# Expert-choice layers: the last expert's round written out, its rows added on chip, the layer norm of all tiles inside it

## What is computed

```python
mix = windowed_gqa_sink(x, ...)            # layer 0
mix = bidir_rglru_block(x, ...)            # layer 1
x = layer_norm(ALPHA * x + mix, ln_mix_g[layer], ln_mix_b[layer])
ffn = expert_choice_moe(x, w_router, w_gate_up, w_down)
x = layer_norm(ALPHA * x + ffn, ln_ffn_g[layer], ln_ffn_b[layer])
```

```python
def expert_choice_moe(x, w_router, w_gate_up, w_down):
    aff = jax.nn.softmax((x @ w_router).astype(jnp.float32), axis=-1)
    gates, idx = lax.top_k(jnp.swapaxes(aff, 1, 2), cap)      # cap = 128 rows for each of 16 experts
    xs = x[bi, idx]
    g, u = jnp.split(jnp.einsum('becd,edf->becf', xs, w_gate_up), 2, axis=-1)
    out = jnp.einsum('becf,efd->becd', jax.nn.silu(g) * u, w_down) * gates[..., None]
    return jnp.zeros_like(x).at[bi, idx].add(out)
```

## Time and profile before

| | |
|---|---|
| median of 3 runs | 4730.37 us (4727.5 to 4732.37) |
| the profiled execution | 4735.36 us, its span 4733.2 us |
| mean granted TensorE clock | 0.949 |
| TensorE busy | 4216.9 us (89%), 23090 records |
| VectorE, ScalarE, GpSimd busy | 1578.3 us (33%), 1068.2 us (23%), 267.2 us (6%) |
| products of layer 0's experts, L2867 and L2893 | 444.5 and 223.4 us |
| products of layer 1's experts, L2867 and L2893 | 444.0 and 223.4 us |

### The profile page before, as it was taken

The page is one execution under the profiler, slowest core; times in us unless marked ns, Lnnn a source line. Parts: engine busy times, 40 slices in busy tenths (PEclk is TensorE's granted clock), DMA queues, the critical chain, the costliest instruction groups (busy, mean ns, idle before and its releaser), DMA issues. The chain is left out here.

```text
span 4733.2 us, 61819 instructions
## 1 busy us (share of the span) xinstructions
PE 4216.9 (89%) x23090; PEld 2186.2 (46%) x23091; DVE 1578.3 (33%) x2933; ACT 1068.2 (23%) x1827; POOL 267.2 (6%) x304
## 2 busy tenths in 40 slices
PE   7899996888999979979899599999699995999995
PEld 4555444776444544434455244444344452444442
DVE  3355354443401232223574410110256444011102
ACT  1155222443200001111363100000246331000002
POOL 0000001221000010010000000000000000000000
PEclk8899998999999989989999799999799997999998
DMA  2040244333212289961104488888511144888884
GB/s 94 22 182 10 62 173 120 82 81 97 86 36 72 85 320 358 358 241 63 46 4 167 159 312 308 311 313 312 167 48 37 54 169 162 309 309 313 312 307 163
DMA packets 416663, 807.16 MB, mean 171 GB/s; under 512 B 140624, under 2 KB 280784, under 8 KB 383568
## 3 DMA queue, kind: packets, MB, share of 16 engines
q1 hardware_dynamic: 387392, 702.80, 42.4%
q0 software_dynamic: 16704, 60.82, 4.7%
q10 hardware_dynamic: 12368, 40.70, 2.2%
HBM read 682.60 MB, written 121.63 MB: 170 GB/s over the span
## 5 line engine op out<-in xcount | busy, mean ns | idle before, releaser
L2867 PE MATMUL ec0e_pg<-ec_wg,ec0e_xT 128*128 128x512 f32 x1024 | 444.5, 595 | 2.1 <-DVE ec0e_xT L2920 2.1
L2867 PE MATMUL ec1e_pg<-ec_wg,ec1e_xT 128*128 128x512 f32 x1024 | 444.0, 594 | 2.1 <-DVE ec1e_xT L2920 2.1
L2867 PEld LDWEIGHTS ec0e_pg<-ec_wg,ec0e_xT 128*128 128x128 f32 x1024 | 195.4, 191 | 248.3 <-issue 248.3
L2867 PEld LDWEIGHTS ec1e_pg<-ec_wg,ec1e_xT 128*128 128x128 f32 x1024 | 195.2, 191 | 248.1 <-issue 248.1
L1385 PE MATMUL mix_pb<-h_h_all,mix_wg 128*128 128x512 f32 x512 | 224.6, 598 | 8.8 <-DMA mix_wg<-in_w_in_dram 8.8
L3151 PE MATMUL lrui_pA<-lrui_xT,lrui_w 128*128 128x512 f32 x512 | 223.7, 597 | 2.6 <-ACT lrui_xT L3225 2.6
L2893 PE MATMUL ec1e_py<-lru_wd,ec1e_hidT 128*128 128x512 f32 x512 | 223.4, 594 | 0.0
L2893 PE MATMUL ec0e_py<-gqa_wd,ec0e_hidT 128*128 128x512 f32 x512 | 223.4, 594 | 0.0
L679 PE MATMUL front_pz<-h_h_all,front_w 128*128 128x512 f32 x480 | 211.6, 599 | 8.8 <-DMA front_ones<-in_head_ones_dram 8.8
L2908 ACT ACTIVATE ec1e_sg<-ec1e_pg 128x512 f32<-128x512 f32 x32 | 19.1, 598 | 649.7 <-PE ec1e_pg L2867 649.7
L2908 ACT ACTIVATE ec0e_sg<-ec0e_pg 128x512 f32<-128x512 f32 x32 | 19.1, 598 | 648.3 <-PE ec0e_pg L2867 648.3
(11 more groups left out here) (550 smaller groups left out, 6251.9 us busy)
## 6 DMA issues: line engine op xcount, KB each, us to landing
ec_wg<-in_moe_w_gate_up_dram SPq DMA_DIRECT2D x256, 1024.0 KB, 6.3
gqa_wd<-in_moe_w_down_dram SPq DMA_DIRECT2D x128, 512.0 KB, 4.4
lru_wd<-in_moe_w_down_dram SPq DMA_DIRECT2D x128, 512.0 KB, 4.4
moe_wb<-in_w_dram SPq DMA_DIRECT2D x32, 1024.0 KB, 14.1
h_h_all<-in_w_dram SPq DMA_DIRECT2D x32, 1024.0 KB, 13.9
wkv_inp<-arrays SPq DMA_DIRECT2D x160, 128.0 KB, 2.8
arrays<-front_out SPq DMA_DIRECT2D x36, 512.0 KB, 5.7
yb<-mlaa_zero SPq DMA_DIRECT2D x1, 16384.0 KB
```

The costliest lines, as they stand in the source:

```text
L2867: return nc.tensor.matmul(pg[:, b, :], xT[:, k, :], wg[:, k, b * HALF:(b + 1) * HALF], start=k == 0, stop=k == KD - 1)
```

## The change

What it does, part by part:
- A new class `Layers` holds what both layers and both of their ends use: the identity, one buffer of eight tiles (`aT`, the former `oT` and `ggT`), the weights `wd`, the norm's vectors `gb`, and the small tiles `rows`, `old`, `place`, `small`, `at`.
- The loop of `choice_phase` runs over 15 experts, and the round of expert 15 (LAST) is written out behind it on every engine. In all rounds TensorE's `turn_hid(1)` now stands in front of k = 2 of the down product. The last round has no `turn_x`, and there is no 17th gather.
- When the scatter of expert 14 has landed, SP loads the eight tiles of `acc_dram`, and GpSimd gathers expert 15's 128 rows of `acc_dram` into `rows` (in layer 0 also into `old`). ScalarE and VectorE norm the eight tiles in place (layer 0: `old` as a ninth) around the steps of the last round; SP stores them. Expert 15's contribution isn't in these tiles.
- VectorE then adds py * gate to `rows` (L3091). In layer 1 these rows are normed into `fixed`, and GpSimd stores them over the output's rows when the tiles' stores have landed. In layer 0 that is done in `lru_mix`: `fixed_rows` norms them, `change` = `fixed` − normed `old`, and TensorE adds the change to `xT` by 16 matmuls with `place`, a matrix of 0 and 1 (a row of it has its 1 at the token of that row). It is made from the new input `steps`. TensorE turns the eight tiles straight from SBUF.
- `norm_phase` is gone, and with it the norm, the reload and the stores in `lru_mix`.

```diff
 choice_phase
+    LAST, R, FIRST, MIDDLE = E2 - 1, NT + 1, 3, 4
+    ALL = NT if end else NT + 1
...
             sync
+                sp.wait_ge(sent, E2)
+                for t in range(NT):
+                    sp.dma_start(tile(t), acc_dram[t * P:(t + 1) * P, :]).then_inc(tile_in[t], 16)
+                for t in range(NT):
+                    sp.wait_ge(o_ready, t + 1)
+                    sp.dma_start(out_dram[t * P:(t + 1) * P, :], tile(t)).then_inc(tile_out, 16)
             gpsimd
-                with pool.Fori(0, E2 // 2) as i:
+                with pool.Fori(0, E2 // 2 - 1) as i:
...
+                gather(1)
+                pool.wait_ge(y_ready, E2)
+                pool.indirect_dma_start(acc_dram, bass.IndirectOffsetOnAxis(ap=ic[0][:, :], axis=0), y[:, :], None, compute_op=ALU.add).then_inc(added, 16)
+                pool.wait_ge(added, 16 * LAST)
+                pool.sem_inc(sent, 1)
+                pool.indirect_dma_start(rows[:, :], None, acc_dram, bass.IndirectOffsetOnAxis(ap=at_last[:, :], axis=0)).then_inc(rows_in, 16)
+                if not end:
+                    pool.indirect_dma_start(old[:, :], None, acc_dram, bass.IndirectOffsetOnAxis(ap=at_last[:, :], axis=0)).then_inc(old_in, 16)
+                pool.wait_ge(x_in, 16 * E2)
+                if end:
+                    pool.wait_ge(fix_ready, 1)
+                    pool.wait_ge(tile_out, NO)
+                    pool.indirect_dma_start(out_dram, bass.IndirectOffsetOnAxis(ap=at_last[:, :], axis=0), fixed[:, :], None).then_inc(fix_out, 16)
+                    pool.wait_ge(fix_out, 16)
             tensor
-                    E.hold(x_in, e * 16 + 32)
-                    turn_x()
-                    turn_hid(1)
+                    if more:
+                        E.hold(x_in, e * 16 + 32)
+                        turn_x()
                     E.hold(y_ready, last(e))
                     for k in range(KD):
+                        if k == 2:
+                            turn_hid(1)
                         E.hold(wd_in[k], now(e, 16))
...
+                with pe.Fori(0, LAST) as e:
+                    one_expert(e, True)
+                one_expert(LAST, False)
             scalar
+                top(LAST)
+                for t in range(FIRST):
+                    stats(t)
+                silu_half(LAST, 0)
+                for t in range(FIRST, MIDDLE):
+                    stats(t)
+                silu_half(LAST, 1)
+                keep_hid(LAST)
+                for t in range(MIDDLE):
+                    roots(t)
+                for t in range(MIDDLE, ALL):
+                    stats(t)
+                    roots(t)
             vector
+                def norm(t, other=None):
+                    dve.wait_ge(sum_done, t + 1)
+                    mean(t, t)
+                    if other is not None:
+                        scaled(other)
+                    mean_squares(t, t)
+                    centred(tile(t), tile(t), t)
...
+                for t in range(FIRST):
+                    norm(t)
+                gated(LAST, 0)
+                for t in range(FIRST, MIDDLE):
+                    norm(t)
+                gated(LAST, 1)
+                keep_hid(LAST)
+                for t in range(MIDDLE, ALL):
+                    norm(t, t - MIDDLE)
+                dve.wait_ge(rows_in, 16)
+                dve.wait_ge(d_used, now(LAST, KD, KD))
+                nc.vector.scalar_tensor_tensor(rows[:, :], py[:, :], gate[:, LAST:LAST + 1], rows[:, :], ALU.mult, ALU.add,
+                                               accum_out=small[:, R, 0:1]).then_inc(rows_ready, 1)
+                rest = range(ALL - MIDDLE, ALL)
+                if end:
...
+                    centred(fixed[:, :], rows[:, :], R)
+                    mean_squares(ALL, R)
+                    scaled(rest[0])
...
+                    nc.vector.scalar_tensor_tensor(fixed[:, :], fixed[:, :], small[:, R, 5:6], gb[:, 1, :], ALU.mult, ALU.add).then_inc(fix_ready, 1)
+                    rest = rest[1:]
+                for t in rest:
+                    scaled(t)
 lru_mix
             tensor
+            def changed(k):
+                if k >= 2:
+                    pe.wait_ge(xT_ready, k - 1)
+                for h in range(2):
+                    m = nc.tensor.matmul(pA[:, 2 * (k % 2) + h, :], change[:, k * P:(k + 1) * P], place[:, halves[h]], start=True, stop=True)
+                m.then_inc(c_psum, 1)
...
-                pe.wait_ge(xT_ready, 4 * h + 4)
+                pe.wait_ge(xT_ready, KD)
...
-            for t in range(4):
+            for t in range(NT):
                 turn(t)
-            branch(0, 0)
...
+            pe.wait_ge(change_ready, 1)
+            for k in range(KD):
+                changed(k)
+            for i in range(2):
+                branch(i, 0)
+                branch(i, 1)
             vector
+            fixed_rows()
+            for k in range(KD):
+                keep_change(k)
```

More of the change, by code:

```diff
@@ L2773, in _, with choice_phase, tile @@
             nc.vector.tensor_copy(gate[:, :], pl[:, E2:2 * E2])
-def choice_phase(nc, name, ident, x_dram, acc_dram, gate, idx, weights, ln_ffn=None, gb=None, gb_in=None):
+def choice_phase(nc, name, layers, x_dram, acc_dram, gate, idx, weights, ln_ffn, out_dram, steps, end):
+    LAST, R, FIRST, MIDDLE = E2 - 1, NT + 1, 3, 4
+    ident, tiles, gb, rows, old, place, small, at_last = (layers.ident, layers.aT, layers.gb, layers.rows, layers.old, layers.place, layers.small,
+                                                          layers.at)
+    gb_in, tile_out = layers.gb_in, layers.tile_out
+    NG = 32 * (2 if end else 1)
+    NO = 16 * NT * (2 if end else 1)
+    ALL = NT if end else NT + 1
+    def tile(t):
+        return tiles[:, t, :] if t < NT else old[:, :]
     with Phase(nc, name) as ph:
@@ L2788, in choice_phase @@
         warm = ph.sb("warm", [P, 1])
+        junk = ph.sb("junk", [P, D])
+        fixed = ph.sb("fixed", [P, D]) if end else None
         pg = ph.ps("pg", [P, 4, HALF])
@@ L2932, in _ @@
                     keep_x()
[L2933 to L2935 removed]
+                    keep_hid(e)
                     V.hold(d_used, now(e, KD))
```

365 lines of the change are left out of this document (167 added, 198 removed).

## The result

The changed kernel takes **4672.19 us** (median of 4 runs, 4668.46 to 4675.37), beside 4731.37 us of the kernel before (4 runs, 4727.5 to 4736.96). The ratio is 0.9874, with a 95% interval of 0.9857 to 0.9891: 59 us faster, between 52 and 68. The forecast was 4685 us, a gain of 45 us. The sign was right; the size was 14 us short. The time lies 0.2 us above the low end of the range, 4672. The kernel before, executed beside it, was itself 1 us longer than the 4730.37 that the forecast started from. By the gain, 59.2 us against the 58.4 of the low end, the result lies 0.8 us outside.

A forecast was written before the change was run, and what follows sets the result against it. TensorE time was taken to bound the expert loops, with idle at two seams and one gap per round; 16.2 + 4.8 + 24.0 = 45.0 us off the median 4730.37 gave 4685 us, range 4672 to 4702.

The forecast's parts named there:

- Part 1: Every round: turn_hid(1) behind the down product's first two steps; TensorE waits for hT_a, 0.54 us less a round, 16.2 us over 30.
- late next: Every round: VectorE's copy of the second half comes after turn_hid(1), needed at k=4; claimed covered with 2.5 us to spare.
- Part 2: Last round: three norms hidden before the first Silu, a fourth between Silus; the rest, 3.3 us each, make VectorE the bound.
- Part 3: Seam from layer 0 to the recurrent mixer, up to its first four products: a gain of 4.8 us.
- I take the half clock, the nearest row: Mixer's start: back-to-back transposes taken at half clock, 8 x 1.95 = 15.6 us, plus 2.1 for the product's half-clock start.
- The rival: Mixer's start: clock rises in the back-to-back transposes, full from the third tile; saves 7.2 us, giving 4678 us; chance 0.24.
- With the same 5.1 it starts at 3398.9: Seam after layer 0: VectorE ends at 3393.8, and the next phase starts 5.1 us later, as it did behind the scatter.
- The loads of gb and place ... cost nothing: Expert loop's start: these loads are covered by TensorE's first product and cost nothing; without that cover 0.5 us each.
- Part 4: End of the program: last operation at 4698.2, indirect store taken at 6.0 us, end at 4709.2; a gain of 24.0 us.
- Behind this point nothing differs: Recurrent mixer after its first four products: TensorE busy nearly without a gap, weights long landed, so no change in time.

## Why the prediction fell short

- **Part 1 was right.** 0.54 us a round was forecast, 0.57 measured (43.93 to 43.36), in all 30 rounds, and ended by hT_a. The second copy, "late next", was covered, as the working had it. What it left out is that in the last rounds VectorE waits in line for that copy: there the new order loses 2.0 us in layer 0 and 1.4 in layer 1 against the old one.
- **Part 2 was right in its mechanism.** Norms hidden ahead of Silu cost nothing, VectorE behind the last product is the bound. A norm with a scaling took 3.0 us, not 3.3 (its lower bound), and the scalings alone 1.40, not 1.48: 2.0 us in layer 0.
- **Part 3 is the step that failed: 4.8 us forecast, 17.7 measured.** Its path was right, three of its terms were mis-sized. "I take the half clock, the nearest row" was wrong: the clock rose within the transposes. That was 5.3 us in them and 2.1 in the product of the change, 7.4 us. The rival had worked out 7.2 by the mechanism that the rows show: the full clock from the third tile on, and then waits for ScalarE's copies (the rows have them from the fifth). "With the same 5.1 it starts at 3398.9" was wrong too: that seam stood behind a transfer that GpSimd had issued, this one behind VectorE, and it took 1.94 us, 3.2 less. Why the one is longer is not shown. With the 2.0 of the norms, and 0.3 by which the last product started sooner, that is the 12.9 us missing. (The 13.9 of its product of the change is 14.1 by its own 32 x 0.44; 13.90 was measured.)
- **"The loads of gb and place ... cost nothing" was wrong.** They have no cover, since they are issued just ahead of the first gather and TensorE waits for that gather. They cost 3.2 us in layer 0. The nearest view was there: in layer 1 of the kernel before, with two such loads ahead, TensorE waited 7.98 us for its gather, in layer 0, with none, 6.58.
- **Part 4 was right to 0.5 us, by errors that cancel.** VectorE ended 1.8 us sooner (55.1 us behind the y step of expert 14, not 56.9), and from there to the end were 12.3 us, not 11.0. The indirect store landed in 3.3 us instead of 6.0, but it started 3.5 us behind VectorE, and 5.5 us followed its landing.
- **"Behind this point nothing differs" was wrong by 5.0 us**, above all the clock drops at two stalls that nobody touched. The result would have been 6 us nearer to the forecast without them, so they are part of the miss, and their cause is open.

The sum by pieces: 45.0 + 0.6 (rounds) + 12.9 (seam) − 3.2 (loads) − 1.1 (start) + 5.0 (recurrent mixer) + 0.5 (end) = 59.7 us.

The Trainium skill (TensorE: Matmul & The Clock Gate, Part 4: PE-mode transpose) says that the full clock doesn't set in for transposes; the durations it measured there are of bf16. The traces disagree for these float32 transposes: 0.62 and then 1.00 in a stretch that has only transposes, and 1.00 throughout where TensorE was kept at work before. The measurement decides; what keeps a clock low here is the pause between transposes, not their kind.

## What to carry to other kernels

A stage that starts cold is priced by how it is packed: rows of the same instructions with pauses between them say little about the same instructions in closed ranks, so where a change removes pauses, weigh the full clock as an equal case. A load that nobody waits for still costs if it is issued just ahead of one that somebody waits for; look at which transfer is first on the path of a new phase. And when two orders of the same work are compared, compare them at both ends of the engine that is the bound there: what is right in a loop that TensorE bounds can be wrong in a last round that VectorE bounds.

## What the runs showed of the hardware that was not expected

- TensorE's clock rose while it did only transposes, back to back (0.50 up to the third tile of eight, 1.00 behind it). With a pause of 1.10 us behind each tile of 1.97 us it stayed at 0.50.
- With three plain loads of 512 KB issued within 1 us of a gather of 128 rows, TensorE waited 9.8 to 10.3 us for it, with two 8.0 to 9.7, with none 6.3 to 6.7.
- A phase change behind VectorE took 1.9 us; behind an indirect scatter of GpSimd, 5.1. An indirect store of 128 rows landed in 3.3 us where the scatter that adds took 6.0, but the end of the program came 5.5 us behind that landing, and 4.0 when SyncE did the waiting. Inside the loop GpSimd went on 0.8 us behind the landing of its own scatter.
- The same stall of 3.24 us, in the same stream, was followed by no loss or by 1.7 or 3.0 us lost to a clock of 0.50, steady for the two kernels that were executed more than once.
